# Expert weights of a mixture-of-experts layer: the two down-product slots of the ring in one transfer of 4 MB

## What is computed

```python
logits = xt @ router_w + router_b
top_val, top_idx = lax.top_k(logits, 4)
gate = softmax(top_val)
# for each expert e and the tokens that chose it:
gu = x_e @ w_gu[e] + b_gu[e]          # 1024 -> 2048
g, up = gu[:, :1024], gu[:, 1024:]
act = (clip(up, -7, 7) + 1) * (min(g, 7) * sigmoid(1.702 * min(g, 7)))
out[tokens of e] += gate * (act @ w_down[e] + b_down[e])   # 1024 -> 1024
```

## Time and profile before

| | |
|---|---|
| median of 3 runs | 1937.54 us (1937.01 to 1938.84) |
| the profiled execution | 1938.65 us |
| its span, first to last instruction | 1936.9 us |
| TensorE busy (with matmul ends modelled) | 1864.7 us, 96% |
| VectorE, ScalarE, GpSimd busy | 768.5, 231.1, 207.3 us |
| DMA, mean over the span | 288 GB/s, 558.10 MB |
| transfers of expert weights | 192 of 2 MB |
| granted TensorE clock, mean | 0.993 |

### The profile page before, as it was taken

The page is one execution under the profiler, slowest core; times in us unless marked ns, Lnnn a source line. Parts: engine busy times, 40 slices in busy tenths (PEclk is TensorE's granted clock), DMA queues, the critical chain, the costliest instruction groups (busy, mean ns, idle before and its releaser), DMA issues.

```text
span 1936.9 us, 23084 instructions
## 1 busy us (share of the span) xinstructions
PE 1864.7 (96%) x8340; PEld 912.3 (47%) x8340; DVE 768.5 (40%) x1594; ACT 231.1 (12%) x466; POOL 207.3 (11%) x397
## 2 busy tenths in 40 slices
PE   7999999999999999999999999999999999999996
PEld 4466777754667777655433333323323333332332
DVE  3553111145535773395633323323223323332334
ACT  1421000014110000231110000000000000000001
POOL 0200000002006868321000000000000000000000
PEclk9999999999999999999899999999999999999999
DMA  8143343241448865225399999999997499999995
GB/s 310 65 172 117 152 159 147 109 186 65 174 189 323 326 264 199 87 87 228 152 428 428 429 429 428 428 428 429 428 429 292 202 429 429 428 428 428 429 429 236
DMA packets 40910, 558.10 MB, mean 288 GB/s; under 512 B 4534, under 2 KB 5430, under 8 KB 6364
## 3 DMA queue, kind: packets, MB, share of 16 engines
q1 hardware_dynamic: 40380, 556.06, 69.5%
q10 hardware_dynamic: 480, 1.37, 0.2%
HBM read 556.35 MB, written 1.06 MB: 288 GB/s over the span
## 4 chain that ended last, share of the span: by engine, by line
PE 65%; DMA 23%; DVE 9%; issue 2%; ACT 1%; POOL 0%; SPq 0%; ACTq 0%; DVEq 0%; POOLq 0%
DMA ring<-in_exp_w 23%; PE PS L1746 15%; PE PS L2048 15%; PE PS L1474 8%; PE PS L1765 8%; PE PS L2079 6%; PE PS L1651 3%; PE PS L1936 1%; PE PS L2034 1%; PE PS L2056 1%; DVE ring L1151 1%; DVE tT L1389 1%; DVE tT L1392 1%; DVE tb L1393 1%; DVE tb L1390 1%
## 5 line engine op out<-in xcount | busy, mean ns | idle before, releaser
L2048 PE MATMUL PS<-ring,tb 128*64 128x512 f32 x2176 | 481.5, 595 | 22.7 <-POOLq L2188 20.2
L2048 PEld LDWEIGHTS PS<-ring,tb 128*64 128x64 f32 x2176 | 150.5, 137 | 349.5 <-issue 295.8
L1746 PE MATMUL PS<-hT,ring 128*128 128x256 f32 x1376 | 300.6, 379 | 0.0
L1746 PEld LDWEIGHTS PS<-hT,ring 128*128 128x128 f32 x1376 | 261.1, 190 | 43.0 <-issue 8.6
L2079 PE MATMUL PS<-ring,tb 128*64 128x512 f32 x1088 | 241.0, 595 | 3.7
L1474 PE MATMUL PS<-ring,hT 128*128 128x512 f32 (+2 forms) x448 | 187.6, 561 | 3.4 <-ACT hT L420 3.3
L1389 DVE TENSOR_SCALAR tT<-PS 128x512 f32<-128x512 f32 x34 | 23.5, 692 | 397.5 <-PE PS L2056 397.5
L1765 PE MATMUL PS<-ring,tT 128*128 128x512 f32 x352 | 154.7, 593 | 0.0
L2079 PEld LDWEIGHTS PS<-ring,tb 128*64 128x64 f32 x1088 | 77.7, 137 | 145.1 <-issue 143.9
L1078 DVE TENSOR_TENSOR tT<-PS,tT 128x512 f32<-128x512 f32 x22 | 15.2, 692 | 270.3 <-PE PS L1746 270.3
L1474 PEld LDWEIGHTS PS<-ring,hT 128*128 128x128 f32 x448 | 81.7, 192 | 72.2 <-issue 60.0
(11 more groups left out here) (449 smaller groups left out, 1584.5 us busy)
## 6 DMA issues: line engine op xcount, KB each, us to landing
ring<-in_exp_w SPq DMA_DIRECT2D x192, 2048.0 KB, 21.2
ring<-in_w_gate_up SPq DMA_DIRECT2D x22, 2048.0 KB, 8.5
ring<-in_ada_w SPq DMA_DIRECT2D x12, 2048.0 KB, 9.3
ring<-in_w_in_part SPq DMA_DIRECT2D x10, 2048.0 KB, 10.1
ring<-in_w_down SPq DMA_DIRECT2D x10, 2048.0 KB, 7.3
ring<-in_w_out SPq DMA_DIRECT2D x6, 2048.0 KB, 8.6
ring<-in_w_in SPq DMA_DIRECT2D x4, 2048.0 KB, 8.1
ring<-in_w_in_part SPq DMA_DIRECT2D x2, 1608.0 KB, 11.8
```

The source lines that it names most:

```text
L1746: ins = pe.matmul(PS[:, 4 + 2 * (i % 2) + part, 256 * f:256 * f + 256], wt[:, k, 256 * part + 128 * f:256 * part + 128 * f + 128], hT[:, k ...
L2048: ins = pe.matmul(PS[64 * h:64 * h + 64, b, :], xg[:, o:o + 64], ring[:, s, w:w + 512], start=k == 0, stop=False, skip_group_check=True)
```

## The change

Slots 4 and 5 of an expert come in one transfer of 4 MB. Its source is an array of its own in which each partition's 32 KB (both slots) lie in one piece; in the ring the two slots of a partition are neighbours as well. In the loop over experts 1 to 31 SyncE waits for `freed[5]` alone before it issues it (whoever raises it has seen the end of the down product, so slot 4 is read as well); for expert 0 it waits for `freed[5]` and `freed[4]`. The transfer raises `landed[5]` alone. `m_w` counts five steps for each item, and TensorE waits for the fifth ahead of the whole down product. Who frees the slots, and when, stays as it is.

```diff
-FIRST_ORDER = (3, 2, 4, 5, 0, 1)
+FIRST_ORDER = (3, 2, 5, 0, 1)
...
-                for slot in FIRST_ORDER if isinstance(e, int) else range(RING):
+                for slot in FIRST_ORDER if isinstance(e, int) else (0, 1, 2, 3, 5):
                     sp.wait_ge(freed[slot], items_before + USES_BEFORE[slot] + 1)
-                    sp.dma_start(ring[:, slot, :], a["exp_w"][e, slot]).then_inc(landed[slot], 16)
+                    if slot == 5:
+                        if isinstance(e, int):
+                            sp.wait_ge(freed[4], items_before + USES_BEFORE[4] + 1)
+                        sp.dma_start(ring[:, 4:6, :].rearrange("p s n -> p (s n)"), a["exp_w_down"][e]).then_inc(landed[5], 16)
+                    else:
+                        sp.dma_start(ring[:, slot, :], a["exp_w_gu"][e, slot]).then_inc(landed[slot], 16)
...
                 for s in range(4):
-                    pe.wait_ge(g.m_w, n * RING + s + 1)
+                    pe.wait_ge(g.m_w, n * (RING - 1) + s + 1)
...
                 for c in range(KC):
                     s = 4 + c // 4
-                    if c % 4 == 0:
-                        pe.wait_ge(g.m_w, n * RING + s + 1)
+                    if c == 0:
+                        pe.wait_ge(g.m_w, n * (RING - 1) + s + 1)
...
-            for slot in range(RING):
+            for slot in (0, 1, 2, 3, 5):
                 pool.wait_ge(landed[slot], LOADS_BEFORE[slot] * 16 + 16)
                 pool.sem_inc(g.m_w, 1)
...
-                for slot in range(RING):
+                for slot in (0, 1, 2, 3, 5):
                     pool.wait_ge(landed[slot], (e + LOADS_BEFORE[slot]) * 16 + 16)
                     pool.sem_inc(g.m_w, 1)
...
-    a["exp_w"] = ew
+    a["exp_w_gu"] = np.ascontiguousarray(ew[:, 0:4])
+    a["exp_w_down"] = np.ascontiguousarray(ew[:, 4:6].transpose(0, 2, 1, 3)).reshape(N_EXPERTS, P, 8192)
```

## The result

The changed kernel takes 1941.23 us (median of 13 runs, 1940.7 to 1942.77) against 1937.67 us before (13 runs, 1936.39 to 1938.96): 3.6 us slower, ratio 1.0020, 95% interval 1.0012 to 1.0027. The profiled execution took 1942.12 us; its span is 1940.1 us, 3.2 us more than before. The forecast was slower by 4.9 us, 1942.4. All times here are medians of executions at the full granted clock (0.99 and more); one execution of one test kernel (`more_second_after`) took 3273 us at a granted clock of 0.567 and is left out.

The account below looks back on a forecast made before the run. Two unbroken DMA transfer streams, with TensorE work between and behind them, were taken to fix the span. Terms 3.3 + 2.3 + 1.1 - 1.8 = +4.9 us gave 1942.4 us, own range 1941 to 1945, 8 in 10 from 1938.8 to 1946.8.

Parts of the forecast that it names:

- hole, first stream: First load of the first transfer stream: the pair, issued at 982.3 us to idle engines, lands at 995.0, +2.3 us.
- hole, second stream: First load after the restart at 1529.2 us: the pair, issued at 1552.1, lands at 1564.5 instead of 1561.2, +3.3 us.
- last items of the streams: Last item of each stream: the down product starts 0.55 us later, waiting for the whole pair, +1.1 us in all.
- pieces of 32 KB, 28 loads: Loads behind the two holes (16 and 12 experts): fewer, longer packets save 0.065 us per pair, -1.8 us.
- Part 1: Expert loop, first load after each idle stretch: the later issue of the pair opens two holes, +2.3 and +3.3 us.
- Part 2: Down product: TensorE waits once for the whole pair; spare 1.83 us hides it except at stream ends, +1.1 us.
- Part 3: Pair transfers in the loop: fewer and longer packets gain between nothing and 0.11 us per pair, taken as 0.065, -1.8 us.
- Parts at nothing: First expert's load, GpSimd's relay with five waits for six, and TensorE's dropped wait: no cost or gain.
- Holes that close by themselves: Rival at the stream restarts: the DMA engines' lead takes up the late issue, leaving -0.7 us, 1936.8; chance 0.18.
- A fixed cost between queued transfers: Rival in the full queue: dropping one transfer per expert gains up to 73 us, 1871; chance 0.04.
- Slower 32 KB pieces: Rival in the pair transfers: 1% slower pieces make the sum +9.4 us, 1947; 3% makes it +15, 1953; chance 0.10.
- A skewed landing: Rival: one engine's share over 1.2 us late lengthens 17 DMA-bound items; chance 0.02, counted within the slower pieces' 0.10.

Follow-up runs that it names:

- more_second_after: Changed kernel with a second item of no tokens added for experts 8 and 26: 1978.2 us, against 1971.6 us for the kernel before with the same items.
- one_wait: Kernel before with only TensorE's wait changed, for slots 4 and 5 ahead of the whole down product: 1939.89 us, +1.6 us, ratio 1.0007.
- late_issue: Kernel before with only slot 4's issue in the loop made late, to the end of the whole down product: 1943.6 us, +5.3 us, ratio 1.0026.
- pieces_16k: Changed kernel with the source keeping the two slots apart, so one 4 MB transfer in 16 KB pieces: 1943.92 us, +5.6 us on the kernel before.
- no_second_after: Changed kernel with tokens of experts 17 and 18 beyond the 64th left out, so no second items: 1898.56 us, against 1898.5 us for the kernel before likewise.

## Why the prediction was right

The mechanism and the sign came out as put, and the holes and the last items were found each by itself. The gain of the pieces is the remainder of the streams in the table; by itself, from the periods, it is 2.1 us. The terms, forecast and found:

| part | forecast | found | by |
|---|---|---|---|
| hole, first stream | +2.3 | +1.7 | pair lands 35.0 us behind the issue of slot 0, slot 5 before 33.3 |
| hole, second stream | +3.3 | +3.0 | 35.0 against 32.0 |
| last items of the streams | +1.1 | +1.3 | 0.70 + 0.64 us |
| pieces of 32 KB, 28 loads | -1.8 | -2.3 | the two streams, less their holes: (0.24 - 1.7) + (2.18 - 3.0) |
| sum | +4.9 | +3.75 | the stretches |

The forecast was 1.3 us too high, the forecast time (1942.4) 1.2: both holes were taken too dear (by 0.6 and 0.3 us) and the gain of the pieces too small (by 0.3 to 0.5), and the last items too cheap by 0.2. The measured 1941.23 lies at the low end of the forecast's own range of 1941 to 1945, and just under its edge of 1941.4 for a time that can be told from no change; 13 runs on each side still tell it (interval 1.0012 to 1.0027).

- *Part 1.* The issues came at 981.8 and 1552.6 us and the landings 12.1 and 12.0 us later (SyncE at L394 of the changed kernel, in two short stretches):

```profile
L394 SPq DMA_DIRECT2D ring<-in_exp_w_down x1: 333/333/333, 981.8 to 981.8; - x1
...
DMA to landing us min/median/max: 12.1/12.1/12.1
...
L394 SPq DMA_DIRECT2D ring<-in_exp_w_down x1: 332/332/332, 1552.6 to 1552.6; - x1
...
DMA to landing us min/median/max: 12.0/12.0/12.0
```

  The standstills of all engines before them are 1.05 us (981.70 to 982.75) and 1.93 us, shorter than the 2 to 3 us put down as a sign, since the first engine runs dry before the last one does (by 1.7 and 1.0 us, from the landing marks of slot 3). I had 12.7 for the first, because I took 7.8 us from idle, halfway between the 8.2 of the first load and the 7.5 of the second, and 12.4 for the second. The 8.2 is a thing of that one transfer (8.0 to 8.4 us in all profiles whose gate/up slots come singly, 7.5 to 8.0 at later restarts); a pair of 32 KB pieces from idle takes 12.0 to 12.1 us at every place of this run and 12.0 to 12.4 in the others. That the load between and the next experts would show no further loss was right: the stretch between lasts 55.10 against 55.11 us, and the engines never stand still inside a stream again.

  Why the first hole is the cheaper one, the prediction put down to a lead of the stream. The landing marks of the single engines say what that lead is: before, they bring in slot 5 of that load 1.7 us apart, and stay 1.7 to 1.9 us apart up to the end of the first stream; in the second stream it is 0.4 us. With the change it is 0.4 to 0.6 us in both. Counted by the first engine to land, both holes cost 2.9 us; the standstill evens the engines out, and TensorE, which waits for the last, gets 1.2 us of the first hole back.
- *Part 2* was mis-sized by 0.1 us per stream: the pair's gain was subtracted, and the time from landing to the start of the product was not looked at. The expectation that the loop's spare 1.83 us take the wait was shown by `one_wait`, whose period did not move.
- *Part 3* was mis-sized as well. Between nothing and 0.11 us per pair I took 0.065; it is 0.08 for the joins (`pieces_16k` against the changed kernel), and what the closing packet adds is too small to be told.
- *Parts at nothing*: the first load is not late (TensorE's first gate/up product starts at 955.0 us, before at 955.5, and waits for VectorE in both), and GpSimd's relay shows nowhere.
- *The rivals.* Holes that close by themselves: excluded by `late_issue`. A fixed cost between queued transfers: excluded by `pieces_16k`, whose one transfer for two leaves the period at 29.38 us. From idle a cost beside the packets shows: 12.0 us for a pair whose packets take 9.7 (8 of 1.217 us on each engine). The Trainium skill ("DMA: Bandwidth & Descriptors", "Anatomy of one DMA") fits a DMA issued by GpSimd as about 2.0 us fixed plus its bytes at 436 GB/s; by that, as an estimate, one transfer for two gains 2 us. The transfers here are issued by SyncE: the 2.3 us from idle are near the fit, the full queue shows nothing of it. Slower 32 KB pieces: the opposite is measured. A row pitch of 32 KB costs nothing here either. A skewed landing: TensorE's wait for the pair is 0.65 us in the last item and in the one before, as it should be without one engine far behind the others.

What the prediction did not see is that the price of a restart depends on the length of the stream behind it. It makes no difference in this kernel, because both streams (16 and 12 loads behind the hole) are long enough. The tests show a hole free in streams of three and five loads, and paid in one of eight.

By these terms a stream pays for its hole and its last item (1.7 + 0.65 in the first, 3.0 + 0.65 us in a later one) with 0.08 us per load: by this estimate it breaks even at 29 and 46 loads. The single stream of `no_second_after`, 30 loads, sits at the first of these numbers. A kernel that joins the pair except behind a restart would by the same estimate come out some 1 us below the kernel before (1.3 - 2.1 to 2.3), less than whole times can tell; it was not tried.

## What to carry over

When two transfers are merged, look for the places where the queue has just run dry, not at the full queue: merging makes the first half wait for the buffer of the second, and what that costs is paid once per restart (here 1.7 to 3.0 us, 3.4 where the two halves stay two transfers), and only if the stream behind it becomes what the engines wait for. In a full queue one issue for two gains nothing; longer contiguous pieces gain a little per joint, here 0.01 us for each 16 KB boundary removed. Small expected gains are better read as differences of stretches between fixed events than as differences of whole times, since untouched code ahead of them scatters by more.

## Not expected

- 32 KB pieces are moved whole, and joining two of 16 KB gains about 10 ns per joint on each engine at 428 GB/s; the period of the expert loop fell from 29.37 to 29.29 us with one pair and to 29.14 us with three.
- A hole of 1.96 us in the transfers of a stream that is bound by them elsewhere cost 0.00 us where only three loads followed.
- The landing marks of the 16 engines stayed 1.5 to 2.0 us apart through the whole first stream where no hole broke its first load, and 0.4 to 0.9 us apart where one did. Why they are apart at first is open.
- The code ahead of the loop ended 3 us apart in the profiles.
